# Moving VectorE's gate weights and residual to later steps of the expert loop

## The reference

```python
hx = _modulate(x, sh2, sc2)
yx = _moe(hx, _route(hx, w_router, router_bias), moe_w1[l], moe_w3[l], moe_w2[l])
x = _layernorm(DEEPNORM_ALPHA * x + g2 * yx, ln_g[l, 1], ln_b[l, 1])
```

## Time and profile before

| | |
|---|---|
| median of 3 runs | 1155.79 us |
| the profiled execution | 1153.72 us |
| its span, first to last instruction | 1152.1 us |
| TensorE busy | 974.1 us (85%) |
| VectorE busy | 336.3 us (29%) |
| ScalarE busy | 222.9 us (19%) |
| GpSimd busy | 247.9 us (22%) |
| mean DMA rate | 287 GB/s |

### The profile page before, as it was taken

The page is one execution under the profiler, slowest core; times in us unless marked ns, Lnnn a source line. Parts: engine busy times, 40 slices in busy tenths (PEclk is TensorE's granted clock), DMA queues, the critical chain, the costliest instruction groups (busy, mean ns, idle before and its releaser), DMA issues.

```text
span 1152.1 us, 24034 instructions
## 1 busy us (share of the span) xinstructions
PE 974.1 (85%) x9166; PEld 548.8 (48%) x9167; DVE 336.3 (29%) x805; ACT 222.9 (19%) x564; POOL 247.9 (22%) x459
## 2 busy tenths in 40 slices
PE   3999999899979999998895769999996859845984
PEld 1544655564455555554553434555544435422543
DVE  1003031752355321221221167222434322101115
ACT  0221111760251111110110013112603101000110
POOL 0200000010016444444332230000001233422232
PEclk9899999989999999999998879999996989977998
DMA  9997292754156876769999995537685999999993
GB/s 336 379 378 287 75 361 79 290 204 198 41 209 236 292 277 231 259 218 355 393 393 403 405 366 212 192 136 258 230 329 223 351 390 398 387 402 414 401 367 112
DMA packets 88435, 330.40 MB, mean 287 GB/s; under 512 B 10416, under 2 KB 12768, under 8 KB 63808
## 3 DMA queue, kind: packets, MB, share of 16 engines
q1 hardware_dynamic: 66592, 282.14, 64.0%
q0 software_dynamic: 20320, 46.43, 11.4%
q10 hardware_dynamic: 1472, 1.12, 0.3%
HBM read 302.66 MB, written 27.00 MB: 286 GB/s over the span
## 4 chain that ended last, share of the span: by engine, by line
PE 72%; DMA 14%; issue 6%; DVE 5%; ACT 2%; SPq 1%; POOL 0%; DVEq 0%; POOLq 0%; ACTq 0%
PE PS L1949 18%; PE PS L1687 16%; DMA W<-in_moe_w 9%; PE PS L1964 8%; PE PS L1851 7%; PE PS L1602 3%; DMA XT<-in_moe_w 3%; PE PS L1938 3%; PE PS L1631 3%; PE PS L1703 3%; PE PS L1956 2%; DMA W<-in_w_ada 2%; PE PS L1801 1%; PE PS L1813 1%; PE PS L1918 1%
## 5 line engine op out<-in xcount | busy, mean ns | idle before, releaser
L1949 PE MATMUL PS<-W,EX 128*32 128x256 f32 x2912 | 180.0, 399 | 65.5 <-DMA W<-in_moe_w 37.0
L1687 PE MATMUL PS<-W,XT 128*128 128x512 f32 (+1 forms) x480 | 188.4, 552 | 0.4 <-ACT XT L830 0.4
L1949 PEld LDWEIGHTS PS<-W,EX 128*32 128x32 f32 x2912 | 96.5, 115 | 133.2 <-issue 82.0
L1687 PEld LDWEIGHTS PS<-W,XT 128*128 128x128 f32 x480 | 90.8, 191 | 93.7 <-issue 91.3
L805 ACT ACTIVATE AT<-EX 64x512 f32<-64x512 f32 x64 | 40.4, 631 | 390.7 <-PE PS L1938 356.1
L1437 DVE COPY EX<-PS 128x256 f32<-128x256 f32 x66 | 28.0, 424 | 294.8 <-PE PS L1949 294.8
L699 POOL TENSOR_TENSOR RSTD<-VAR,HALF 128x1 f32<-128x1 f32 (+1 forms) x24 | 18.3, 765 | 444.2 <-DVE VAR L1120 444.2
L1949 PE MATMUL PS<-RAB,EX 128*32 128x256 f32 x640 | 82.3, 415 | 27.6 <-DMA XT<-in_moe_w 18.7
L730 POOL DMA_DIRECT2D y_rows<-AT x128 | 63.6, 499 | 165.1 <-DVE AT L1448 83.8
L1964 PE MATMUL PS<-W,AT 128*32 128x256 f32 x1472 | 89.0, 382 | 0.6 <-DVE AT L1444 0.6
L730 POOL DMA_DIRECT2D y_rows<-EX x120 | 59.5, 496 | 132.7 <-DVE EX L1450 62.5
(11 more groups left out here) (242 smaller groups left out, 1056.1 us busy)
## 6 DMA issues: line engine op xcount, KB each, us to landing
W<-in_moe_w SPq DMA_DIRECT2D x65, 2048.0 KB, 19.7
W<-in_w_ada SPq DMA_DIRECT2D x24, 2048.0 KB, 12.1
RAB<-in_moe_w SPq DMA_DIRECT2D x10, 2048.0 KB, 21.1
XT<-in_moe_w SPq DMA_DIRECT2D x10, 2048.0 KB, 25.2
H<-in_moe_w SPq DMA_DIRECT2D x10, 2048.0 KB, 21.3
W<-in_w_in SPq DMA_DIRECT2D x7, 2048.0 KB, 18.6
W<-in_w_out SPq DMA_DIRECT2D x4, 2048.0 KB, 20.0
EX<-xg_rows POOLq DMA_DIRECT2D x128, 64.0 KB, 5.7
```

The lines of the kernel that those rows point to most:

```text
L1687: mm = pe.matmul(ps[:, 0:cw], XT[:, k, P * t:P * t + P], w[:, k, :], start=(k == 0), stop=(k == KD - 1))
L1949: mm = pe.matmul(UP_PS[o:o + ROWS, 0:256], rows, w[:, 256 * a:256 * a + 256], start=(k == 0), stop=(k == KD - 1), tile_position=(0, o))
```

## The change

The gate weights move from step 0 to step 1. In the first layer the residuals of tiles 0, 1, and 2 with 3, which lay in steps 0, 1 and 2, now lie like this: tile 0 in step 1, tiles 1 and 2 in step 2, tile 3 in step 4, ahead of that step's `marks`. In the last layer the residuals stay in steps 1 and 2. `affine` is still counted up by the residual of the last tile: in the first layer that is now in step 4 instead of step 2.

```diff
                 def beside(n):
 
-                    if n == 0:
+                    if n == 1:
                         wp = WK2[:, 0:T, :]
...
-                    for t in {4: ((0,), (1,), (2, 3)), 2: ((), (0,), (1,))}[T][n]:
+                    for t in {4: ((), (0,), (1, 2), (), (3,)), 2: ((), (0,), (1,), (), ())}[T][n]:
                         for hf in range(2):
                             read(dve, ("xT", L, t, hf))
                         ins = residual(L, 0, t)
...
                     product()
+                    beside(n)
                     if n < 3:
-                        beside(n)
                         continue
                     if n == 3:
                         last_rows = shares()
```

## The result

The changed kernel takes 1164.95 us, the median of 9 runs (1159.31 to 1170.14), beside 1155.79 us for the kernel before (9 runs, 1152.75 to 1160.05). The ratio is 1.0085, 95% interval 1.0062 to 1.0108: 7 to 12.5 us slower. The profiled execution took 1166.51 us with a span of 1164.9 us, 12.8 us more than that of before, so this pair of profiles differs by more than the medians do (9.2 us).

A forecast was written before the change was run, and what follows sets the result against it. It took TensorE as the bound (72% of the chain), VectorE costing only where TensorE waits. 9.2 us (step 1's 1.3 included) + 1.8 for the clock = 11.0, on 1155.79: 1166.8 us; range 1164 to 1169, 8 in 10 1160 to 1170.5.

The forecast's parts named there:

- The late `affine` holds back GpSimd's queue, and block 7 with it: First layer, steps 4 to 6: late vector loads delay block 7's rows; 9.2 us lost, 1.3 of step 1 included.
- the last layer's range: Landing time of the same pair of row loads behind the vectors in the last layer: 12.2 to 13.6 us.
- Step 1, 1.3 us: First layer: the added gate weights delay `copy_up`, `rows_out` and the `up` behind by 1.3 us, between 0 and 1.3.
- Step 0, no gain: First layer: VectorE relieved of 3.72 us; gain between 0 and 0.4 us, taken as 0.
- The clock: After TensorE's wait of 8 us its granted clock is lower: 1.3 to 2.4 us, taken as 1.8.
- It carries to the end: From step 6 on: weight loads move with TensorE, so the 11 us delay carries whole.
- The rival of absorption: After 604: the delay comes out of TensorE's 11.7 us wait for weights; time stays at 1155.8 us; chance 0.08.
- The rival of equal halves: Vectors get half of the DMA, block 7 is in time, only step 1's 1.3 us stay: 1157.1 us; chance 0.07.
- A landing within 8.8 us: Block 7's rows land sooner, as in this layer before: 7.1 us lost, 1162.9 us; chance 0.18.
- more than one wait: Blocks 8 and 9 are late too: another 4 us, 1171 us; chance 0.07.
- Last layer, no cost: Gate weights in step 1 disappear in 3.19 us of idling before the next `copy_up`; `affine` stays in step 2; cost 0.

The follow-up runs named there:

- tile-3 run: The kernel before with only the residual of tile 3 moved to step 4, gate weights and other tiles unmoved: ratio 1.0074 (1.0048 to 1.0099).
- wait-alone run: The changed kernel with GpSimd's wait for `affine` in place but both vector loads behind the rows of blocks 7 and 8: ratio 0.9980 (0.9960 to 1.0000).
- gate-weights run: The kernel before with only the gate weights moved to step 1, all residuals as before: ratio 1.0022 (0.9995 to 1.0049).
- rows-first: The changed kernel with GpSimd issuing the rows of blocks 7 and 8 before its `affine` wait and vector loads: ratio 0.9987 (0.9971 to 1.0004).

## Why the prediction was right

It forecast 1166.8 us and slower; the medians say 1164.95, a loss of 9.2 us where the sum had 11.0. The two profiles differ by 12.8. That the sum lies so near the medians is partly luck: in this pair of profiles one of its terms was short by 3.2 us, and some 3 us more, in the last layer, belong to none of them. By its own steps:

**The late `affine` holds back GpSimd's queue, and block 7 with it: right, and shown.** Taking the rows out from behind it removes the loss; moving only tile 3, on the same chip, makes nearly all of it. The issue of L687 came at 389.16 instead of 385.7, later by what steps 1 to 3 had lost more than I had priced; from the end of the residual on, the steps of the sum fit. The pair landed within 11.8 us where I took 12.2; my reason for the lower end of the last layer's range, fewer loads outstanding, is tested by nothing. The wait by the sum was 401.7 - 393.8 = 7.9 us; it was 8.21. TensorE's `turn_rows` of step 6 came 12.7 us later than before, where the sum had 9.2: the difference is that of steps 1 to 3.

**What I had not seen in that term is how it divides.** The prediction spoke of the late count and of the vectors ahead as one. The runs show that the lateness alone is covered but for 0.85 us of wait, and that the two loads in front add 3.4 and 2.6 us and the entry into the loop 1.4.

**Step 1, 1.3 us: the mechanism was right, the sum of this profile was short.** `copy_up(2)` came 3.2 us later: 1.3 of the gate weights, and 1.9 because the product before it came at 365.73 instead of 363.85, with the rows of block 3. Their issue had waited 5.63 us for the scatter instead of 4.26. This is not the change's: the tile-3 run and the wait-alone run waited 4.1, the gate-weights run 5.5. Then an `up` ran 1.7 us longer at the lower clock, which I had priced only behind step 6. With both, product 4 was 4.5 us late instead of 1.3. That is of this one execution; what the step costs over the timed runs is open (-0.6 to 5.7 us by the gate-weights run).

**Step 0, no gain: the bound of 0.4 us was wrong, and the zero right by another way.** `up(2)` started 0.9 us earlier than in the kernel before, and then TensorE waited 1.70 us for block 3. The idle time before `up(2)` is 0.85 to 1.11 us in all six profiles with the gate weights in step 1, and 1.84 to 2.13 us in the four with them in step 0. In the rows-first and the wait-alone run block 3 was in time and the gain stayed: from `up(1)` to `up(5)` they took 28.1 and 27.9 us, the two others of their chip 30.6 and 30.4, in which an `up` also ran some 1.7 us longer at the lower clock. So part of what these two runs won back may be a gain here, and not the loss undone.

**The clock: 1.8 us forecast, 1.6 measured.** `down` took 3.48 us instead of 1.93 after the wait, and the `up` behind it 3.66 again.

**It carries to the end: nearly.** The next `up` was 13.3 us later than before (409.75 for 396.43). The weight load issued at 605.07 before was at 616.66, 11.6 us later. The missing 1.7 us are those of an `up` of 5.35 us that the kernel before had at 433.81 at the lower clock, and for which the changed one has 3.66. The waits for weights from 604 to 700 were 1.9 us shorter (10.3 for 11.7, and 5.6 for 6.1), and the loads of SyncE that stood at 710.70 and 895.48 came 10.8 and 9.3 us later. The rival of absorption falls. In the last layer the distance of the two profiles grew again, to 12.1 us at SyncE's load at 931.12 (919.01 before). There TensorE idled 5.43 us before an `up` at 911.72, with no releaser named. In all eight experiments the longest wait of this kind there (890 to 945) is 5.4 to 6.1 us too, and three of them have the gate weights in step 0; in the profile before (885 to 935) it is 3.4. So some 3 of the 12.8 us (12.1 - 9.3) are most likely of this one profile of before, and not of the change.

**The rival of equal halves falls.** It wanted both vectors to land 5.7 us after their issue and the pair of rows within 4.3; the vectors took 9.1 and 12.7 us, and the pair 9.2 to 11.8. In the changed kernel, from 389 to 404, GpSimd's queue moved 1.34 MB with 25.0% of the engines' time and SyncE's 4.47 MB with 75.3%: a quarter again, as in the earlier trace rows. The Trainium skill, "DMA: Bandwidth & Descriptors", section "Queues, rings and completion order", has the turns go by packets. The shares measured are not equal halves of the time.

**The two other rivals fall as well.** A landing within 8.8 us did not come (11.8). Nor did more than one wait: block 8 was staged at 406.87, and `turn_rows` of step 7 began at 413.27 without a wait.

**Last layer, no cost: not tested by itself.** Behind its residual of step 1 VectorE had no idle time in this profile, where I had read 3.19 us of cover, but no wait of TensorE for VectorE's copies stands there.

## What to carry to other kernels

When work on one engine is moved later, ask first which count it ends with and who sits behind that count in an order of its own: here 2.4 us of a vector engine that idles 70% of the time, moved by two steps, made a queue 12.4 us late (389.16 for 376.76). Then ask what stands between that count and the next thing somebody needs, because a late wait with small work behind it may be covered while the same wait with 1 MB in front of a 128 KB load is not. Where a wait is for housekeeping, put it behind the loads that the critical engine will ask for next. And where an experiment is to bound a term, look in its trace whether the term arises there at all.

## What the runs showed of the hardware

The granted clock fell after quite short waits and not after others: an `up` took 5.35 us behind waits of 1.70 and 1.92 us close together, and 3.66 us in the gate-weights run behind waits of 1.64 and 1.92 us. Each fall cost 1.7 us (5.35 for 3.66), more than the 1.3 us that the prediction gave step 1.

The same pair of 64 KB loads of block 7 landed within 2.1 us when issued 1.8 us ahead of the weight loads of its stretch (384.10, 385.87, rows-first run), and within 7.3 us when issued 6.0 us behind them (389.74, 383.70, wait-alone run), with no vectors ahead of it on its queue in either. With one vector ahead it took 10.1 us, with two 11.8.

GpSimd's wait for the scatter of rows ahead of block 3, which none of these edits touches, was either about 4.1 to 4.4 us or 5.3 to 5.6 us from one profile to the next, and moved step 1 with it.
